# A causal mask moved from TensorE's accumulation to GpSimd multiplies, and the order of a stage's tail dealt out anew

## What is computed

```python
def stick_breaking(q, k, v, q_pos, k_pos, bias):
    z = einsum('bqhd,bkhd->bhqk', q, k) * (DH_A ** -0.5) + bias
    mask = k_pos[None, :] < q_pos[:, None]
    log_beta = log_sigmoid(z)
    log_keep = where(mask, log_sigmoid(-z), 0.0)
    later = cumsum(log_keep, axis=3, reverse=True) - log_keep
    att = where(mask, exp(log_beta + later), 0.0)
    return einsum('bhqk,bkhd->bqhd', att, v)
```

## Time and profile before

| | |
|---|---|
| median of 3 runs | 3948.12 us (3945.47 to 3951.25) |
| profiled execution, time | 3945.47 us |
| profiled execution, span | 3943.8 us |
| mixers stage, first scores to last write of mix | 601.79 to 1393.68 us |
| PE busy in the whole span | 3584.2 us, 91% |
| POOL busy in the whole span | 349.6 us, 9% |
| mean granted TensorE clock | 0.951 |

### The profile page before, as it was taken

One profiled execution on the slowest core, in us unless ns is written; L12 is line 12 of the kernel. 1 busy time (PEld: TensorE's weight loads), 2 busy tenths in 40 slices (PEclk: granted clock), 3 DMA queues, 4 the chain that ended last, 5 costly groups with the idle time before them and its releaser, 6 DMA issues. The chain is left out here.

```text
span 3943.8 us, 53913 instructions
## 1 busy us (share of the span) xinstructions
PE 3584.2 (91%) x20160; PEld 3161.1 (80%) x20160; DVE 1738.8 (44%) x3292; ACT 1110.2 (28%) x2008; POOL 349.6 (9%) x917
## 2 busy tenths in 40 slices
PE   5999677999899988999999988988879899999997
PEld 4999664656565587999999987987559799999997
DVE  5444313455555435443443456324662543443446
ACT  2434222333333334111111124212233411111113
POOL 0000103343333200000000000000000000000000
PEclk9999897999999998999999998998779899999998
DMA  4222443121211021111111111222320111111111
GB/s 121 97 96 96 133 140 88 36 70 33 76 25 42 16 89 37 43 45 43 43 43 43 43 27 51 95 68 91 114 85 27 49 43 43 43 43 43 43 43 51
DMA packets 306622, 241.64 MB, mean 61 GB/s; under 512 B 76322, under 2 KB 271206, under 8 KB 306490
## 3 DMA queue, kind: packets, MB, share of 16 engines
q1 hardware_dynamic: 294794, 197.03, 17.1%
q0 software_dynamic: 11696, 42.87, 2.9%
HBM read 181.27 MB, written 58.59 MB: 61 GB/s over the span
## 5 line engine op out<-in xcount | busy, mean ns | idle before, releaser
L451 PE MATMUL ffn_ps<-ffn_in_hi,ffn_w_hi 128*128 128x368 f32 x2112 | 704.0, 333 | 34.3 <-DVE ffn_w_lo L894 22.0
L452 PE MATMUL ffn_ps<-ffn_in_lo,ffn_w_hi 128*128 128x368 f32 x2112 | 702.3, 333 | 0.0
L453 PE MATMUL ffn_ps<-ffn_in_hi,ffn_w_lo 128*128 128x368 f32 x2112 | 700.3, 332 | 0.0
L451 PEld LDWEIGHTS ffn_ps<-ffn_in_hi,ffn_w_hi 128*128 128x128 f32 x2112 | 400.3, 190 | 40.8 <-DVE ffn_w_lo L894 23.1
L452 PEld LDWEIGHTS ffn_ps<-ffn_in_lo,ffn_w_hi 128*128 128x128 f32 x2112 | 400.2, 189 | 0.5
L453 PEld LDWEIGHTS ffn_ps<-ffn_in_hi,ffn_w_lo 128*128 128x128 f32 x2112 | 400.5, 190 | 0.0
L451 PE MATMUL ffn_ps<-ffn_h_hi,ffn_w_hi 128*128 128x368 f32 x1056 | 354.0, 335 | 10.7 <-DVE mix L967 9.9
L453 PE MATMUL ffn_ps<-ffn_h_hi,ffn_w_lo 128*128 128x368 f32 x1056 | 349.1, 331 | 0.0
L452 PE MATMUL ffn_ps<-ffn_h_lo,ffn_w_hi 128*128 128x368 f32 x1056 | 348.1, 330 | 0.0
L967 DVE TENSOR_TENSOR mix<-ffn_ps,mix 128x368 f32<-128x368 f32 x480 | 256.2, 540 | 191.1 <-PE ffn_ps L453 190.5
L838 ACT ACTIVATE ffn_w_hi<-ffn_w_raw 128x1024 fp32r<-128x1024 f32 x132 | 136.2, 1046 | 463.2 <-PE ffn_ps L453 463.2
(11 more groups left out here) (488 smaller groups left out, 6576.9 us busy)
## 6 DMA issues: line engine op xcount, KB each, us to landing
ffn_w_raw<-in_w_ffn_gate_dram SPq DMA_DIRECT2D x44, 512.0 KB, 3.9
ffn_w_raw<-in_w_ffn_up_dram SPq DMA_DIRECT2D x44, 512.0 KB, 3.9
ffn_w_raw<-in_w_ffn_down_dram SPq DMA_DIRECT2D x44, 512.0 KB, 3.6
ab_w_raw<-in_w_in_ab_dram SPq DMA_DIRECT2D x27, 512.0 KB, 3.9
rwkv_prep<-xT POOLq DMA_DIRECT2D x4, 2208.0 KB, 7.4
qkv_proj<-qk_out_sb POOLq DMA_DIRECT2D x16, 552.0 KB, 3.0
atts_k_page<-in_cache_k_dram SPq DMA_DIRECT2D x32, 256.0 KB, 2.8
atts_v_page<-in_cache_v_dram SPq DMA_DIRECT2D x32, 256.0 KB, 3.0
```

The lines of the kernel that those rows point to most:

```text
L451: pe.matmul(out, w_hi, x_hi, start=first, stop=False)
L452: pe.matmul(out, w_hi, x_lo, start=False, stop=False)
L453: return pe.matmul(out, w_lo, x_hi, start=False, stop=last)
```

## The change

The mask is no longer part of the scores. Scores of diagonal steps are one product; `not_earlier` and its building are gone. Instead POOL multiplies the 128x128 (or 16x16) square on the diagonal by `earlier` (1 or 0), in place, twice in each diagonal step: sp after DVE has written it (part 1 of t = n + 1, ahead of `later`), and w after ACT's exp (part 2 of t = n + 3). Two new semaphores, sp_masked and att_masked, count them. PE waits for the first ahead of sums(n) and for the second ahead of values(n).

The plan loses its special tail: the last 10 items get the weights of their kinds (mean, var and state_out 1, the others 0), which make 7 in place of 30, and the total is 502 in place of 525.

```diff
+    diag_at = [sum(st[6] for st in steps[:n]) for n in range(NS)]
...
-    norm = r_steps.index(("mean", NPAIR - 1, 0))
-    shares = list(accumulate(shares[:norm] + [3] * (len(r_steps) - norm)))
+    shares = list(accumulate(shares))
...
         @block.gpsimd
-            pool.tensor_scalar(not_earlier[:, :], c["earlier"][:, :], BIG, -BIG, ALU.mult, ALU.add).then_inc(once_zero, 1)
-            pool.wait_ge(once_zero, 5)
+            pool.wait_ge(once_zero, 4)
...
+            def mask(n, x, ready, masked_x):
+                pool.wait_ge(ready, n + 1)
+                keys, lo, width, k0 = shape(n)
+                pool.tensor_tensor(x[0:keys, lo:lo + keys], x[0:keys, lo:lo + keys], c["earlier"][0:keys, 0:keys],
+                                   ALU.mult).then_inc(masked_x, 1)
+
             def attention_steps():
                 for t, part in s_steps:
                     n = t - 1
                     if part == 1 and 0 <= n < NS:
                         keys, lo, width, k0 = shape(n)
+                        if steps[n][6]:
+                            mask(n, sp_[:, n % 2, :], sp_done, sp_masked)
                         if not steps[n][7]:
                             before = width if first[n] else shape(n - 1)[1]
                             pool.wait_ge(sp_done, n + 1)
+                            if steps[n][6]:
+                                pool.wait_ge(sp_masked, diag_at[n] + 1)
...
+                    n = t - 3
+                    if part == 2 and 0 <= n < NS and steps[n][6]:
+                        mask(n, w[:, n % 2, :], att_done, att_masked)
                     yield
...
         @block.tensor
-                mm = pe.matmul(att[0:keys, Z, lo:width], k_in[:, hh, k0:k0 + keys],
-                               q_in[:, i % 2, q0 + lo:q0 + width], start=True, stop=not diag, skip_group_check=True)
-                if diag:
-                    mm = pe.matmul(att[0:keys, Z, lo:lo + keys], c["ident"][0:keys, 0:keys],
-                                   not_earlier[0:keys, 0:keys], start=False, stop=True, skip_group_check=True)
-                mm.then_inc(z_mm, 1)
+                pe.matmul(att[0:keys, Z, lo:width], k_in[:, hh, k0:k0 + keys],
+                          q_in[:, i % 2, q0 + lo:q0 + width], start=True, stop=True).then_inc(z_mm, 1)
 
             def sums(n):
                 keys, lo, width, k0 = shape(n)
                 pe.wait_ge(sp_done, n + 1)
+                if steps[n][6]:
+                    pe.wait_ge(sp_masked, diag_at[n] + 1)
...
             def values(n):
...
                 pe.wait_ge(att_done, n + 1)
+                if diag:
+                    pe.wait_ge(att_masked, diag_at[n] + 1)
```

More of the change, by code:

```diff
@@ L2088, in attention_and_rwkv @@
         ln_w, gn_eps = s.sb("ln_w", [P, NPAIR]), s.sb("gn_eps", [P, 1])
-        masks, not_earlier = s.sb("masks", [P, 3, P]), s.sb("not_earlier", [P, P])
+        masks = s.sb("masks", [P, 3, P])
         s_masks = s.sb("s_masks", [TS, 3, TS])
@@ L2122, in attention_and_rwkv @@
                                                         ("z_mm", "z_scaled", "z_capped", "exp_done", "log_done"))
-        sp_done, summed, later_mm = (s.sem(n) for n in ("sp_done", "summed", "later_mm"))
-        w_done, att_done, pv_mm, out_done = (s.sem(n) for n in ("w_done", "att_done", "pv_mm", "out_done"))
+        sp_done, sp_masked, summed, later_mm = (s.sem(n) for n in ("sp_done", "sp_masked", "summed", "later_mm"))
+        w_done, att_done, att_masked, pv_mm, out_done = (s.sem(n) for n in
+                                                         ("w_done", "att_done", "att_masked", "pv_mm", "out_done"))
         once_in, once_zero, once_done = s.sem("once_in"), s.sem("once_zero"), s.sem("once_done")
@@ L2633, in _ @@
             pe.sem_inc(pe_done, 1)
-            pe.wait_ge(once_zero, 5)
+            pe.wait_ge(once_zero, 4)
             weave(plan, rwkv_steps(), attention_steps())
@@ L2809, in _ @@
             dve.wait_ge(once_in, 16)
-            dve.wait_ge(once_zero, 11)
+            dve.wait_ge(once_zero, 10)
             dve.wait_ge(empty, 1)
```

## The result

The changed kernel takes **4004.43 us** (median of 4 runs, 4000.39 to 4005.97), the kernel before 3949.68. The ratio is **1.0141 [1.012, 1.0161]**: slower by some 55 us. The forecast was 3956 in a range of 3937 to 3978, so the sign was right, its size far too small, and the time lies outside the range. The 3949.68 is a median of four executions, one of which took 4167.71 us and is left out of the ratio; without it the median is 3948.12.

A forecast was written before the change was run, and what follows sets the result against it. The prediction took TensorE to bound the mixers stage's long middle, with a chain bounding its end. Terms -14 + 7 + 3 + 1 + 12 - 1 = +8 on 3945.47 gave 3953.5, stated as 3956 against the median; range 3937 to 3978.

The forecast's parts named there:

- The mask matmuls, -14: Attention's 72 diagonal steps: removing their mask matmuls saves TensorE 14 us (14 to 20), priced start to start.
- Two masks on GpSimd, +7: Diagonal steps: late masks hold up sums or values, 5.4 us, plus 2 us for lost clock; 0 to 20.
- signs of being wrong: In the profile after: sums waiting over 15 us, DVE two-input operations over 10% slower, or tail over 10 us shorter, nothing late.
- The start: Stage start: sums stall 9 us, absorbed by later idle time; denser order -2, GpSimd masks +1, in all -1.
- Block inversions +3: Masks before and between parts of the block inversions on GpSimd delay TensorE's waits for them by 3 us (0 to 7).
- DVE contention +1: DVE and GpSimd slow each other; 144 more GpSimd instructions cost 1 us (0 to 4), mostly hidden.
- rival (e): DVE slowed on TensorE's path by a fourth of GpSimd's new 63 us: +16 for +1, 3971 us; chance 0.03.
- The order, +12: Last three tiles to stage end: moved work +13, tail shortened 7.4, net +6; gap +2, clock +4; +4 to +19.
- +2: Ahead of the tail: the group waiting until 1332.02 gets less attention work before it, so its gap grows 2 us.
- Up to three tiles: Tail: thinly filled last tiles may run at 1.2 GHz, 3.4 us more each; 0 to +7, taken as +4.
- 2 + 4 us: Lower clock: 2 us for stalls from late masks, 4 us for the last tiles in the tail.
- (d): GpSimd's in-order queue makes block inversions hold sums; a third of 20 groups lose 3 us and clock: +30, 3978; chance 0.05.

The follow-up runs named there:

- masks_order_before: The changed kernel with the old line of tail weights put back, both masks still on GpSimd; 3978.36 us, 1.008 against the kernel before.
- values later: Both masks on GpSimd in the old order, values issued one step later with a third buffer of w; 3957.34 us, 1.0026 against the kernel before.
- a weight of 5: The kernel before with weight 5 in place of 3 for the ten tail items; 3955.29 us, 1.0016 against the kernel before.

## Why the prediction was wrong

**The mask matmuls, -14: right in the work, half of it kept.** The stage's work fell by 14.4 to 14.6. With nothing put in their place the time fell by 8: what was left behind was a little more idle time and low clock. The prediction took a microsecond of matmul as a microsecond of time.

**Two masks on GpSimd, +7: the step that failed.** It read: "For the second mask, between exp and values, four are late by 1.2 us together." The prediction does not say how it got there; asking only whether GpSimd is busy with an instruction when exp ends gives three steps and 0.8 us in the trace of before, close to it. But that is not when the mask starts: it starts when all that is queued ahead of it is through, and in the changed order that is several instructions of a block inversion and the first mask and `later` sum of the step two further on, each bound to its own input. Rows 5 already hold a case. The exp of step 59 ends at 1008.27 and its values start at 1014.43:

```profile
1008.07 0.20 ACT L2724 ACTIVATE mixers_w<-mixers_w 16x16 f32<-16x16 f32 x1
1014.43 0.25 PE L2619 MATMUL attp_ps<-mixers_w,mixers_v 16*64 16x16 f32 x2 [0.84 <-issue]
```

Its second mask stands behind the `later` sum of step 61, which GpSimd ends at 1018.27: 4 us too late. Doing this for all 72 steps, with the times of the kernel before and the queue's order of masks_order_before, gives 17 late steps in 10 places; with the largest lateness of each place, 29 us. The trace of before thus held an answer close to what was measured. Measured: 15 waits, 38.0 us in the changed kernel and 12, 32.9 us in the old order; with the second mask 29 - 4 = 25 us go, with a step more for it (values later) 20. The first mask was judged by its place in TensorE's queue, a whole step ahead of sums, and away from the start it was mostly on time; at the start its stall was called absorbed, and against no mask it costs 12 us alone. None of the prediction's signs of being wrong looked at values. Together the terms for the masks on GpSimd and what they press on, 7 + 3 + 1, were 11; measured against the kernel without any mask it is 37.

**The start.** A stall came, but 11.1 us and before values, for the second mask, where 9 before sums, for the first, were predicted:

```profile
618.39 0.40 ACT L2737 ACTIVATE mixers_w<-mixers_w 128x256 f32<-128x256 f32 x1
629.63 0.45 POOL L2301 TENSOR_TENSOR mixers_w<-mixers_w,earlier 128x128 f32<-128x128 f32 x1
630.23 1.08 PE L2632 MATMUL attp_ps<-mixers_w,mixers_v 128*64 128x256 f32 x2 [11.10 <-POOL mixers_w L2301]
658.18 2.05 PE L2415 MATMUL rwkv_ps<-mixers_tu,mixers_nn 128*128 128x128 f32 x8 [9.15 <-issue]
```

It was called absorbed. The idle time ahead of the tile did shrink from 15.37 to 9.15, but the tile starts 6.0 us later, in a stage that starts 2.3 later (604.1 for 601.8): 3.7 passed on, where -1 stood in the sum.

**Block inversions +3, DVE contention +1: small, as said.** With the first mask alone the waits for inverted blocks are 26.7 us in 7, with 26.0 in 8 before: no growth. In the changed kernel, where values wait first, they are fewer. DVE's maximum, the operation of the earlier trace rows, has the mean 555 ns after and 558 before:

```profile
L2908 DVE TENSOR_TENSOR mixers_sp<-mixers_zs,mixers_zc 128x512 f32<-128x512 f32 (+5 forms) x120 | 66.6, 555 | 0.1
```

So rival (e), DVE slowed on the path, is refuted. The page that it went by (the Trainium skill, GPSIMD Engine Reference, 4.1 Engine selection) says that elementwise work with two inputs belongs on VectorE, and that GpSimd is about twice slower. The runs agree in direction, 441 ns on GpSimd and 278 on DVE, 1.6 times. But 0.16 us less for a mask does not explain some 23 us (+29 against +5.5); on DVE the second mask was never waited for longer than 1.3 us, where on GpSimd it was up to 10.8, for what stands ahead of it in the queue.

**The order, +12: the right sign, less than half the size.** The prediction had the work moved ahead at +13, and the tail shortened by 7.4. The move cost +27.8 ahead of ("x", 36): about 13.7 of work, 7 more idle and 7 more clock loss. The tail gave back 1.6: it lost 14.9 of work, but idled 7.9 more and lost 5.4 more by the clock. So the term's two wrong parts are the idle time and clock ahead of the tail, where +2 stood, and the tail's own, -7.4 with +4 for the clock. "Up to three tiles" at the lower clock was the right thought with too low a price: in the changed kernel the clock was 0.50 from 1425 on, normalization included. Its first and last mean there take 1.44 and 1.57 us for the 0.89 of the earlier trace rows:

```profile
1434.57 1.44 PE L2578 MATMUL rwkv_ps<-mixers_y,pair_ones 128*128 128x368 f32 x2
...
1448.94 1.57 PE L2578 MATMUL rwkv_ps<-mixers_tmp,pair_ones 128*128 128x368 f32 x2 [0.90 <-ACT mixers_tmp L2707]
```

**The clock, in for 2 + 4 us, was some 40.** Granted clock 0.50 held for 71.7 us of the stage before, with 12 falls to it, and for 176.5 after, with 19. The prediction priced it at one place of the tail and added 2 us for all stalls.

**The rivals.** (d) had the mechanism, GpSimd's in-order queue holding TensorE behind block inversions, on sums where it was values; it gave +30 for it, and the masks in the old order cost +29. It got 0.05 on GpSimd's busy share, 35 to 43%, which says nothing on how much stands ahead of one instruction. The two large losses, masks and order, were never put together in one case, and that is why the range ended at 3978.

**What stays open.** Whether masks and order also act on each other is not shown: in the profiled executions 7 of the stage's 60.4 us are in neither half, but by the medians the halves add up to 3 us more than the whole. Idle time and clock loss were never changed apart from each other: that the pauses lower the clock rests on the stretches around 944 us and on both growing together, and not on a run that held one still; three of the 19 falls came after 6 us of work almost without a pause. Of the 17 us that the masks on GpSimd still cost with values later, the waits of sums and GpSimd's extra time are the likely parts, not split by a run. And why a weight of 5 doesn't gain is only partly seen.

## What to carry to other kernels

- An instruction put on an in-order engine starts when all ahead of it in that queue is through. For each one list what is queued ahead and when the last of it ends, and compare that with when the consumer would start; the engine's busy share (10% of this kernel, 40% of the stage) and "was it busy at that moment" both miss it. A step more between producer and consumer, with one more buffer, took away 20 us here.
- On an engine near its full use, look for the price of a pause twice: in the idle time, and in work after it at half the clock. Here 36.8 us more idle came with some 40 us more clock loss.
- In this kernel the tail's cover went with a higher clock. Moving 46 matmuls out of a 42 us tail shortened it by 1.6 us while its clock fell from 0.87 to 0.62, and 28 us came on where they went.

## What was not expected of the hardware

- The lower clock can last long. In the changed kernel it held from 1425 to 1469 without a break, with TensorE busy 21.84 of 44 us; the tail of 40.8 us ran at a mean of 0.62, that of before at 0.87. The Trainium skill (TensorE: Matmul & The Clock Gate, Part 1: The HAM clock gate) ties the clock to how busy TensorE has been of late; the stretches around 944 us agree, 1.40 busy us of 6 ahead of the one at 0.72; those around 1076.9 do not show it, with TensorE busy throughout ahead of the fall.
- Taking out work may lower the clock: without any mask the stage had 82.3 us at 0.50, with the mask matmuls 71.7. That is one execution each; over all of them the mean granted clock is 0.947 (10) and 0.949 (25), too near to call it shown.
- 63 us more of GpSimd work in the stage left DVE's maximum, an operation of two inputs, unchanged in mean (555 and 558 ns), although a single one had taken about twice its time beside GpSimd.
